# Forget-gate columns as row dot products on VectorE, from a second load of x

## The chip, the cores and the metric

One core of one Trainium2 chip. The time is that of one execution on the device, in microseconds; the profile is of one execution of its own. TensorE multiplies, VectorE (DVE), ScalarE (ACT) and GpSimd (POOL) work elementwise, and SyncE (SP) only issues DMAs. Each has an in-order queue of its own; they meet at semaphores.

## The reference

Two layers of a sequence trunk, T = 2048 tokens of width 1024, float32. What matters here:

```
h    = x * rsqrt(mean(x*x) + eps) * norm_g        # per token
proj = h @ w_in                                   # 1024 x 3972, 15 column groups
fq, fk, fv, ff, fg, r_pre, ... = split(proj, (256, 256, 256, 4, 256, 896, ...))
log_f = log_sigmoid(ff + b_f)                     # 4 columns: one forget gate per head
Ft    = cumsum(log_f, over the tokens)            # used in the first attention
...                                               # four mixers, each gated
x = x + mixed @ w_out
```

The group `ff` has four columns, at rows 768 to 771 of the transposed projection that the kernel keeps.

## The kernel before

Every layer projects first. TensorE forms `projT` (3972 x T) in tiles of 128 output columns of `w_in`. To keep float32 accuracy with the fast float32 form, weights and activations are split in a high and a low part (`w_hi`, `w_lo`, `h_hi`, `h_lo`), and each product is three matmuls (lines 147, 151 and 153). A tile is four blocks of 512 tokens, a block 8 x 3 = 24 matmuls into one of two PSUM accumulators `acc`. Class `Projector` (lines 74 to 171) has a method per engine:

- `act_load` fetches a tile's weights into `raw` (512 KB), issued by ScalarE, when `raw` is free; `act_split` rounds them to `w_hi` when the buffer `w_hi[q]` is free; `pool_weights` subtracts to `w_lo` on GpSimd (line 115).
- `pe_tile` runs the matmuls. The first one of a tile frees the other weight buffer, so the next but one tile's weights are split during it. Before each block it waits (line 143) until `acc` is free.
- `evacuate` (lines 158 to 165) copies `acc` to `stage`: a wait and a decrement for the accumulator, a wait and a decrement for the stage buffer, the copy, a drain that raises `acc_free`.
- `sp_store` writes the stage to DRAM (256 KB).

`phase_project` is the first stage of a layer. SP loads x in 16 tiles of 128 tokens into four buffers `xb` (line 214). ScalarE sums the squares and forms the factor `rst` per token (line 256 to 260), VectorE scales xb in place (line 363), TensorE turns it (line 313), VectorE applies the gain (line 371), ScalarE and GpSimd split h. Beside that run the first two weight tiles. Then comes `tiles`: on every engine the same order of six more tiles, written out by hand, the first four in a loop of two rounds, then the last one of the group `r_pre`, and then the four columns of `ff` (`R_FF`, with m = 4). In `tiles` VectorE only evacuates, GpSimd and ScalarE only prepare weights. At the end SP waits for the last stores (line 239); a barrier closes the stage.

`phase_rwkv_prep` and `phase_rwkv_scan` project the other tiles between their own work, one tile per unit, with the weight buffer alternating (`q`, `1 - q`). Their plans of how many matmuls go in at which point aren't touched. The attention and output stages follow; they read `projT` from DRAM.

## Time and profile before

| | |
|---|---|
| time, median of 3 | 3059.63 us (3056.31 to 3061.36) |
| profiled execution, first to last instruction | 3053.4 us |
| mean granted clock of TensorE | 0.978 |
| TensorE busy | 2901.2 us, 95% |
| VectorE busy | 1441.2 us, 47% |
| ScalarE busy | 1079.7 us, 35% |
| GpSimd busy | 1064.3 us, 35% |

The page gives no time of the profiled execution other than its span; the timed runs are 3 to 8 us above that span, 6.2 at the median. The first layer's `tiles` run from about 82 to 213 us of the span, the second layer's from about 1606 to 1737. Matmuls are pipelined: a record of about 0.39 us starts every 0.227 us. "DVEq" and "PEq" are waits in the engine's own queue.

### The profile page before, as it was taken

How to read it: one execution, taken by the hardware profiler on the slowest of the kernel's cores; microseconds unless marked ns; L12 is line 12 of the kernel's file. 1: busy time of each engine (PE TensorE's matmuls, PEld its weight loads, DVE VectorE, ACT ScalarE, POOL GpSimd, SP SyncE). 2: the span in 40 equal slices, each digit the busy share in tenths (PEclk: the TensorE clock that was granted, in tenths of full speed). 3: DMA queues.
4: the chain of work that ended last, by engine and by line, in shares of the span. 5: the costliest groups of instructions: out<-in, count | busy, mean ns of one | idle time of the engine just before them, and what ended most of it. 6: DMA issues, size and time to landing. Idle time of an engine off the chain costs nothing. (4 is left out here: it accounts for less than half of the span.)

```text
span 3053.4 us, 68189 instructions
## 1 busy us (share of the span) xinstructions
PE 2901.2 (95%) x26644; PEld 2137.6 (70%) x26644; DVE 1441.2 (47%) x2152; ACT 1079.7 (35%) x2188; POOL 1064.3 (35%) x998
## 2 busy tenths in 40 slices
PE   7999989999999899989989999899999998998899
PEld 6867877777777644467768678677777776444677
DVE  5117743323233387767461177432233323877674
ACT  5004433333333234633150044333333332346331
POOL 5101113355555523632151011233555555236221
PEclk9999999999999899999999999999999998999999
DMA  5225543344444341266342255433444443512663
GB/s 159 76 71 166 162 128 95 109 128 131 128 129 128 115 150 40 84 196 205 113 157 76 75 161 161 131 97 109 127 128 132 129 124 115 150 40 84 195 205 114
DMA packets 440642, 383.21 MB, mean 126 GB/s; under 512 B 130696, under 2 KB 369544, under 8 KB 440328
## 3 DMA queue, kind: packets, MB, share of 16 engines
q1 hardware_dynamic: 369576, 345.06, 37.1%
q10 hardware_dynamic: 70752, 33.85, 4.2%
q8 instruction: 211, 3.46, 0.5%
q14 instruction: 103, 0.84, 0.1%
HBM read 239.62 MB, written 139.23 MB: 124 GB/s over the span
## 5 line engine op out<-in xcount | busy, mean ns | idle before, releaser
L147 PE MATMUL ch_acc<-h_hi,ch_w_hi 128*128 128x512 f32 (+1 forms) x2032 | 813.6, 400 | 25.0 <-PEq L144 25.0
L153 PE MATMUL ch_acc<-h_hi,ch_w_lo 128*128 128x512 f32 (+1 forms) x2032 | 821.5, 404 | 0.0
L151 PE MATMUL ch_acc<-h_lo,ch_w_hi 128*128 128x512 f32 (+1 forms) x2032 | 817.7, 402 | 0.0
L147 PEld LDWEIGHTS ch_acc<-h_hi,ch_w_hi 128*128 128x128 f32 (+1 forms) x2032 | 377.6, 186 | 113.0 <-issue 29.1
L151 PEld LDWEIGHTS ch_acc<-h_lo,ch_w_hi 128*128 128x128 f32 (+1 forms) x2032 | 377.1, 186 | 95.9 <-issue 9.8
L153 PEld LDWEIGHTS ch_acc<-h_hi,ch_w_lo 128*128 128x128 f32 (+1 forms) x2032 | 376.9, 185 | 88.0 <-issue 0.3
L115 POOL TENSOR_TENSOR ch_w_lo<-ch_raw,ch_w_hi 128x1024 fp32r<-128x1024 f32 (+1 forms) x62 | 149.8, 2416 | 641.2 <-POOLq L114 641.2
L1814 ACT ACTIVATE fx_prob<-fx_ST 128x512 f32<-128x512 f32 (+3 forms) x320 | 153.9, 531 | 189.6 <-PE fx_ST L1661 95.9
L2069 PE MATMUL so_acc<-ea_wo_hi,so_m_hi 128*128 128x512 f32 x512 | 209.6, 409 | 7.5 <-DVEq L2174 3.8
L2070 PE MATMUL so_acc<-ea_wo_hi,so_m_lo 128*128 128x512 f32 x512 | 204.2, 399 | 0.0
L2071 PE MATMUL so_acc<-ea_wo_lo,so_m_hi 128*128 128x512 f32 x512 | 204.2, 399 | 0.0
L867 POOL TENSOR_SCALAR rs_qx<-rs_qx,rs_gain 128x256 f32<-128x256 f32 x112 | 103.5, 924 | 281.5 <-ACT rs_qr L1160 264.0
L164 ACT COPY ch_stage<-ch_acc 128x512 f32<-128x512 f32 x192 | 112.3, 585 | 227.8 <-ACTq L163 227.6
L1590 POOL TENSOR_TENSOR fx_sump<-fx_sump,fx_prob 128x1024 f32<-128x1024 f32 (+2 forms) x60 | 126.6, 2109 | 188.2 <-ACT fx_prob L1814 186.9
L1728 DVE TENSOR_REDUCE fx_nm<-fx_SS 128x2 f32<-128x1024 f32 (+3 forms) x160 | 166.4, 1059 | 46.9 <-PE fx_SS L1637 32.0
L164 DVE COPY ch_stage<-ch_acc 128x512 f32<-128x512 f32 (+1 forms) x64 | 44.1, 689 | 259.8 <-DVEq L163 259.8
L110 ACT ACTIVATE ch_w_hi<-ch_raw 128x1024 fp32r<-128x1024 f32 x64 | 65.9, 1029 | 243.0 <-ACTq L109 243.0
L2004 POOL TENSOR_TENSOR so_m_lo<-so_y,so_m_hi 128x512 fp32r<-128x512 f32 x58 | 79.6, 1372 | 191.7 <-ACT so_m_hi L1944 187.1
L1717 DVE TENSOR_TENSOR fx_sumd<-fx_sumd,fx_prob 128x1024 f32<-128x1024 f32 (+3 forms) x72 | 129.2, 1795 | 11.8 <-ACT fx_prob L1814 5.0
L2069 PEld LDWEIGHTS so_acc<-ea_wo_hi,so_m_hi 128*128 128x128 f32 x512 | 97.7, 191 | 35.9 <-DVEq L2174 8.4
L2071 PEld LDWEIGHTS so_acc<-ea_wo_lo,so_m_hi 128*128 128x128 f32 x512 | 97.2, 190 | 23.8
L2070 PEld LDWEIGHTS so_acc<-ea_wo_hi,so_m_lo 128*128 128x128 f32 x512 | 97.8, 191 | 21.6
(286 smaller groups left out, 4812.5 us busy)
## 6 DMA issues: line engine op xcount, KB each, us to landing
projT<-ch_stage SPq DMA_DIRECT2D x248, 256.0 KB
ch_raw<-w_in ACTq DMA_DIRECT2D x62, 512.0 KB, 5.4
pj_xb<-x SPq DMA_DIRECT2D x32, 512.0 KB, 4.2
so_stage<-x SPq DMA_DIRECT2D x64, 256.0 KB, 3.0
rp_pre<-projT SPq DMA_DIRECT2D x16, 899.5 KB, 7.6
rs_qx<-projT SPq DMA_DIRECT2D x112, 128.0 KB, 3.3
rs_cs<-rope SPq DMA_DIRECT2D x48, 256.0 KB, 3.6
so_cv<-projT SPq DMA_DIRECT2D x42, 258.0 KB, 3.8
```

What stands on the lines that cost most here:

```text
L115: (G or self.nc.gpsimd).tensor_tensor(self.w_lo[q][:, :, 0:m], self.raw[:, :, 0:m], self.w_hi[q][:, :, 0:m].bitcast(F32), ALU.subtract).th ...
L147: ins = M(acc, self.w_hi[q][:, k, 0:m], self.h_hi[:, k, cols], start=(k == 0), stop=False)
L151: M(acc, self.w_hi[q][:, k, 0:m], self.h_lo[:, k, cols], start=False, stop=False)
L153: ins = M(acc, self.w_lo[q][:, k, 0:m], self.h_hi[:, k, cols], start=False, stop=(k == KC - 1))
L164: copy(self.stage[e][0:m, :], self.acc[e][0:m, :]).then_inc(self.stage_rdy[e], 1)
L1590: G.tensor_tensor(sump[R % 2][:, :, lo:TB], sump[R % 2][:, :, lo:TB], prob[nt % NP][:, :, lo:TB], ALU.add).then_inc(s["add_p"], 1)
L1717: V.tensor_tensor(sumd[R % 2][:, :, lo:TB], sumd[R % 2][:, :, lo:TB], prob[i % NP][:, :, lo:TB], ALU.add).then_inc(s["add_d"], 1)
L1728: V.tensor_reduce(nm[p][:, :, t, c:c + 1], SS[ns % 2][:, :, 0:width(t, c)], AX.X, ALU.max, negate=True).then_inc(s["m_rdy"], 1)
L1814: A(prob[nt % NP][:, h, lo:TB], ST[h][:, lo:TB], ACT.Exp).then_inc(s["p_rdy"], 1)
L2069: M(a, m_hi[e][:, c, rows], wo_hi[:, c, cols], start=(i == 0), stop=False)
L2070: M(a, m_lo[e][:, c, rows], wo_hi[:, c, cols], start=False, stop=False)
L2071: ins = M(a, m_hi[e][:, c, rows], wo_lo[:, c, cols], start=False, stop=(i == KC - 1))
```

## The change

The small tile is gone from `tiles`, which now has five tiles, unrolled. Two new inputs are prepared on the host from the inputs: `gate_w`, the four columns of `w_in` laid out as rows of 1024, and `gains`, `norm_g` as a row. SP broadcasts both to all 128 partitions once the first pass of x is nearly through, and then loads x a second time, tile by tile, into the same four buffers. On VectorE `gate_w` is multiplied by the gain, and one `scalar_tensor_tensor` per token tile and column multiplies x by the weights and sums over the row (`accum_out`); its elementwise output goes to a PSUM tile that nobody reads. `dots_done(n)` spreads the 64 dots over blocks 1 to 18: three or four behind each evacuation. The sums are multiplied by `rst`, turned by TensorE (64 columns), copied and stored by four small DMAs into the four rows of `projT`.

Because one tile less runs, the weight buffers are exchanged from there on: `q` for `1 - q` in both later stages. The diff, without the parts that only hand the new inputs down:

```diff
@@ -190,28 +190,36 @@
         NZ = (R_RG - R_PRE) // 128
         zero = P.sb("zero", [128, NZ, PAD])
         pt = [P.ps(f"pt{q}", [128, KC, 128]) for q in two]
-        names = ("c_in", "p_in", "c_rdy", "z_st", "r_rdy", "x_rdy", "pt_rdy", "hg_rdy", "hi_rdy", "lo_rdy", "lo3_rdy")
+        gw, gr = P.sb("gw", [128, NH, DM]), P.sb("gr", [128, 1, DM])
+        fl, ft = P.sb("fl", [128, NH, NT]), P.sb("ft", [NH * NT, 128])
+        dots = P.ps("dots", [128, DM])
+        names = ("gw_in", "dot_rdy", "fl_rdy", "ft_rdy", "f_rdy", "f_st", "c_in", "p_in", "c_rdy", "z_st", "r_rdy", "x_rdy", "pt_rdy", "hg_rdy", "hi_rdy", "lo_rdy", "lo3_rdy")
         s = {n: P.sem(n) for n in names}
         x_in = [P.sem(f"x_in{q}") for q in range(NX)]
         block = ctx.enter_context(nc.Block())
         rows = [R_PRE, R_PRE + 128]
         assert NZ == 7
+        rest = [R_PRE + 128 * i for i in range(2, NZ)]
+
         def tiles(eng, body):
-
-            with eng.Fori(0, 2) as i:
-                for q in two:
-                    body(i * 256 + (R_PRE + 128 * (q + 2)), q, i * 256 + (R_PRE + 128 * (q + 3)))
-            body(R_RG - 128, 0, R_FF, 128, NH)
-            body(R_FF, 1, R_FQ, NH, 128)
+            for i, row in enumerate(rest):
+                body(row, i % 2, (rest + [R_FQ])[i + 1])
+
+        def dots_done(n):
+
+            return -(-NT * NH * n // (NB * len(rest) - 2))
         @block.sync
         def _(sp):
             def load(t):
-                if t >= NX:
+                if NX <= t < NT + NX:
                     sp.wait_ge(s["pt_rdy"], t - NX + 1)
-                sp.dma_start(xb[t % NX][:], x[t * 128:(t + 1) * 128, :]).then_inc(x_in[t % NX], 16)
+                if t >= NT + NX:
+                    sp.wait_ge(s["dot_rdy"], NH * (t - NT - NX + 1))
+                tok = t % NT * 128
+                sp.dma_start(xb[t % NX][:], x[tok:tok + 128, :]).then_inc(x_in[t % NX], 16)
             load(0)
             sp.dma_start(ident[:], consts[:, 0:128]).then_inc(s["c_in"], 16)
@@ -221,6 +229,11 @@
             for t in range(2, NT + 8):
                 if t < NT:
                     load(t)
+                if t == NT:
+                    sp.dma_start(gr[:], gains[l:l + 1].to_broadcast([128, 1, DM])).then_inc(s["gw_in"], 16)
+                    sp.dma_start(gw[:], gate_w[l:l + 1].to_broadcast([128, NH, DM])).then_inc(s["gw_in"], 16)
+                if NT < t <= NT + NX:
+                    load(t - 1)
                 if t == NT - 1 and l == 0:
                     sp.wait_ge(s["c_rdy"], 1)
                     for r0, r1 in ((R_PRE, R_RG), (R_SK, R_SG), (R_CB, R_CG)):
@@ -231,10 +244,18 @@
                     if t == BT * b + 9 + 2 * n and 0 <= b < NB:
                         J.sp_store(sp, rows[n], b, 128, n)
-            def body(row, q, follows, m=128, after=128):
+            def body(row, q, follows):
                 for b in range(NB):
-                    J.sp_store(sp, row, b, m)
+                    J.sp_store(sp, row, b)
+                    n = rest.index(row) * NB + b
+                    for t in range(NX, NT):
+                        if dots_done(n) >= NH * (t - NX + 1) > dots_done(n - 1):
+                            load(NT + t)
             tiles(sp, body)
+            sp.wait_ge(s["f_rdy"], 1)
+            for j in range(NH):
+                sp.dma_start(projT[R_FF + j:R_FF + j + 1, PAD:PAD + T].rearrange("j (t p) -> (j t) p", p=128), ft[NT * j:NT * (j + 1), :]).then_inc(s["f_st"], 16)
+            sp.wait_ge(s["f_st"], 16 * NH)
             for q in two:
                 sp.wait_ge(J.stage_st[q], 16)
             if nz:
@@ -281,11 +302,11 @@
                 if t == 8:
                     J.act_load(act, R_PRE + 256)
-            def body(row, q, follows, m=128, after=128):
-                J.act_split(act, q, m)
-                J.act_load(act, follows, after)
+            def body(row, q, follows):
+                J.act_split(act, q)
+                J.act_load(act, follows)
             tiles(act, body)
-            J.act_split(act, 0)
+            J.act_split(act, 1)
         @block.gpsimd
         def _(pool):
@@ -298,8 +319,8 @@
                 pool.drain().then_inc(s["lo_rdy"], 1)
                 if t == 4:
                     J.pool_weights(pool, 1)
-            tiles(pool, lambda row, q, follows, m=128, after=128: J.pool_weights(pool, q, m))
-            J.pool_weights(pool, 0)
+            tiles(pool, lambda row, q, follows: J.pool_weights(pool, q))
+            J.pool_weights(pool, 1)
         @block.tensor
         def _(pe):
@@ -345,10 +366,12 @@
             for _ in tile[1]:
                 pass
-            def body(row, q, follows, m=128, after=128):
-                for _ in J.pe_tile(pe, q, m):
+            def body(row, q, follows):
+                for _ in J.pe_tile(pe, q):
                     pass
             tiles(pe, body)
+            pe.wait_ge(s["fl_rdy"], 1)
+            nc.tensor.transpose(dots[0:NH * NT, 0:128], fl[:].rearrange("p j t -> p (j t)"), ident[:]).then_inc(s["ft_rdy"], 1)
         @block.vector
         def _(v):
@@ -380,10 +403,30 @@
                     if t == BT * b + 7 + 2 * n and 0 <= b < NB:
                         J.evacuate(v, V.tensor_copy, b, 128, n)
-            def body(row, q, follows, m=128, after=128):
+            def dot(n):
+                t, j = divmod(n, NH)
+                if j == 0:
+                    v.wait_ge(x_in[t % NX], 16 * ((NT + t) // NX + 1))
+                V.scalar_tensor_tensor(dots[:], xb[t % NX][:], 1.0, gw[:, j], ALU.mult, ALU.mult, accum_out=fl[:, j, t:t + 1])
+                v.drain().then_inc(s["dot_rdy"], 1)
+
+            def body(row, q, follows):
                 for b in range(NB):
-                    J.evacuate(v, V.tensor_copy, b, m)
+                    J.evacuate(v, V.tensor_copy, b)
+                    n = rest.index(row) * NB + b
+                    if n == 0:
+                        v.wait_ge(s["gw_in"], 32)
+                        for j in range(NH):
+                            V.tensor_tensor(gw[:, j], gw[:, j], gr[:, 0], ALU.mult)
+                        v.drain()
+                    for i in range(min(dots_done(n - 1) if n else 0, NT * NH), min(dots_done(n), NT * NH)):
+                        dot(i)
+                    if n == NB * len(rest) - 2:
+                        V.tensor_tensor(fl[:], fl[:], rst[:].rearrange("p (o t) -> p o t", o=1).to_broadcast([128, NH, NT]), ALU.mult)
+                        v.drain().then_inc(s["fl_rdy"], 1)
             tiles(v, body)
+            v.wait_ge(s["ft_rdy"], 1)
+            V.tensor_copy(ft[:], dots[0:NH * NT, 0:128]).then_inc(s["f_rdy"], 1)
 PREP_FILL = (("th", 16), ("lora", 24), ("ssk", 20), ("bs", 36))
...
-                J.act_split(act, 1 - q)
+                J.act_split(act, q)
...
-            units(pool, lambda i, q, row, follows: J.pool_weights(pool, 1 - q))
+            units(pool, lambda i, q, row, follows: J.pool_weights(pool, q))
-                tile = J.pe_tile(pe, q)
+                tile = J.pe_tile(pe, 1 - q)
...
-                            J.pool_weights(pool, (t + 1) % 2)
+                            J.pool_weights(pool, t % 2)
...
+        "gate_w": np.ascontiguousarray(a["w_in"][:, :, R_FF:R_FF + NH].transpose(0, 2, 1)), "gains": a["norm_g"][:, None, :],
```

## Rows read from the trace of the kernel before

The timeline's rows give the start, the length, the engine, the line, the operation with output <- input, and in brackets the idle time ahead and what ended it. A queue's own name (DVEq, PEq) stands for a wait in it.

**Rows 1.** The page: engines' busy time, and TensorE's granted clock in 40 slices.

```profile
PE 2901.2 (95%) x26644; PEld 2137.6 (70%) x26644; DVE 1441.2 (47%) x2152; ACT 1079.7 (35%) x2188; POOL 1064.3 (35%) x998
...
PEclk9999999999999899999999999999999998999999
```

**Rows 2.** Stretches: length, busy us (instructions) of five engines, granted clock, DMA share, GB/s.

```profile
87.80:109.60 21.80, 21.80 (x97) 18.04 (x97) 2.78 (x5) 1.06 (x1) 4.19 (x2) 1.00 0.23 74
...
191.10:213.40 22.30, 22.01 (x96) 7.87 (x93) 2.76 (x5) 1.06 (x1) 2.41 (x1) 1.00 0.03 13
...
216.70:220.40 3.70, 3.64 (x10) 2.84 (x11) 0.00 (x0) 1.01 (x1) 0.00 (x0) 0.56 0.70 215
```

**Rows 3.** Timeline, DVE: start us, length us, line, tiles, [idle before it].

```profile
87.83 0.69 DVE L164 COPY ch_stage<-ch_acc 128x512 f32<-128x512 f32 x1 [4.75 <-DVEq L163]
93.26 0.69 DVE L164 COPY ch_stage<-ch_acc 128x512 f32<-128x512 f32 x1 [4.75 <-DVEq L163]
...
191.18 0.69 DVE L164 COPY ch_stage<-ch_acc 128x512 f32<-128x512 f32 x1 [4.75 <-DVEq L163]
196.73 0.68 DVE L164 COPY ch_stage<-ch_acc 4x512 f32<-4x512 f32 x1 [4.86 <-DVEq L163]
...
213.37 0.68 DVE L164 COPY ch_stage<-ch_acc 4x512 f32<-4x512 f32 x1 [4.87 <-DVEq L163]
```

**Rows 4.** Groups of DVE by shape: count | busy us, mean ns | idle us.

```profile
L371 DVE TENSOR_TENSOR pj_hg<-pj_pt,pj_pars 128x1024 f32<-128x1024 f32 x32 | 39.1, 1221 | 22.4 <-PE pj_pt L313 21.9 <-issue 0.4
...
L2155 DVE SCALAR_TENSOR_TENSOR so_g<-ea_vs,so_g 128x1024 f32<-128x1024 f32 x16 | 18.9, 1222 | 1.2
...
L533 DVE COPY rp_pend<-rp_lw 128x8 f32<-128x8 f32 x16 | 2.6, 164 | 0.0
```

**Rows 5.** Timeline, DVE, where a drain or a wait lies between instructions.

```profile
224.27 2.03 DVE L495 TENSOR_TENSOR rp_dif<-rp_pre 128x1792 f32<-128x1792 f32 x1 [0.20 <-DVEq L494]
226.49 2.86 DVE L500 SCALAR_TENSOR_TENSOR rp_xs<-rp_dif,rp_pars,rp_pre 128x256 f32<-128x256 f32 x7 [0.20 <-DVEq L498]
229.49 0.62 DVE L506 TENSOR_SCALAR rp_kkr<-rp_xs,rp_pars 128x256 f32<-128x256 f32 x2
230.18 0.69 DVE L508 TENSOR_TENSOR rp_dif<-rp_kkr 128x512 f32<-128x512 f32 x1
```

**Rows 6.** Timeline, DVE, two large instructions merged.

```profile
2856.18 2.36 DVE L2155 SCALAR_TENSOR_TENSOR so_g<-ea_vs,so_g 128x1024 f32<-128x1024 f32 x2
```

**Rows 7.** Timeline, ACT: a sum over the row and its read-out.

```profile
59.78 1.04 ACT L256 ACTIVATE pj_sq<-pj_xb 128x1024 f32<-128x1024 f32 x1
60.73 0.19 ACT L256 ACTIVATION_READ_ACCUMULATOR pj_sq<-pj_xb 128x1 f32 x1
60.98 0.29 ACT L258 ACTIVATE pj_rst<-pj_ms,pj_eps 128x1 f32<-128x1 f32 x1
```

**Rows 8.** Timeline, POOL beside the stage.

```profile
87.19 2.40 POOL L115 TENSOR_TENSOR ch_w_lo<-ch_raw,ch_w_hi 128x1024 fp32r<-128x1024 f32 x1 [6.51 <-POOLq L114]
105.48 2.40 POOL L115 TENSOR_TENSOR ch_w_lo<-ch_raw,ch_w_hi 128x1024 fp32r<-128x1024 f32 x1 [15.89 <-POOLq L114]
```

**Rows 9.** Timeline, all engines, where POOL and DVE meet.

```profile
241.41 0.69 DVE L538 SCALAR_TENSOR_TENSOR rp_ta<-rp_cmp,rp_kkr 128x512 f32<-128x512 f32 x1
...
241.61 2.72 POOL L115 TENSOR_TENSOR ch_w_lo<-ch_raw,ch_w_hi 128x1024 fp32r<-128x1024 f32 x1 [46.68 <-POOLq L114]
...
242.02 2.87 DVE L539 SCALAR_TENSOR_TENSOR rp_tb<-rp_ta,rp_kkr 128x512 f32<-128x512 f32 x1
```

**Rows 10.** Timeline, SP and TensorE at the end of the stage, first layer.

```profile
214.14 0.25 SPq L171 DMA_DIRECT2D projT<-ch_stage  x1
216.42 0.42 SPq L449 DMA_DIRECT2D rp_pre<-projT  x1
...
216.76 0.47 PE L147 MATMUL ch_acc<-h_hi,ch_w_hi 128*128 128x512 f32 x1 [3.65 <-PEq L144]
```

**Rows 11.** Line 214, the loads of x: issues, and their time to landing.

```profile
DMA to landing us min/median/max: 3.2/4.2/6.6
```

More of the change, by code:

```diff
@@ L171, in sp_store, with phase_project @@
         sp.dma_start(self.projT[bass.ds(r, m), PAD + b * TB:PAD + (b + 1) * TB], self.stage[e][0:m, :]).then_inc(self.stage_st[e], 16)
-def phase_project(nc, l, x, par, consts, projT, h_hi, h_lo, J):
+def phase_project(nc, l, x, par, gate_w, gains, consts, projT, h_hi, h_lo, J):
     with ExitStack() as ctx:
@@ L979, in body @@
             def body(t, row, e):
-                tile = J.pe_tile(pe, e)
+                tile = J.pe_tile(pe, 1 - e)
                 def fill(stage):
@@ L1196, in body @@
                 if nxt is not None:
-                    J.act_split(act, 1 - e)
+                    J.act_split(act, e)
                 for sa, xa, f1, f2 in (("s6a", "x4_a", "s6", "s7"), ("s8a", "x5_a", "s8", "s9")):
@@ L2198, in _, with hybrid_trunk @@
                 add_x(n, 3)
-def hybrid_trunk(nc, x, w_in, w_out, par, lora, consts, masks, rope, out, layers=L, debug=None):
+def hybrid_trunk(nc, x, w_in, w_out, par, gate_w, gains, lora, consts, masks, rope, out, layers=L, debug=None):
     def dram(n, shape):
@@ L2214, in hybrid_trunk @@
                 J = Projector(Phase(nc, ctx, f"ch{l}", closes=False), nc, l, w_in, h_hi, h_lo, projT)
-                phase_project(nc, l, source, par, consts, projT, h_hi, h_lo, J)
+                phase_project(nc, l, source, par, gate_w, gains, consts, projT, h_hi, h_lo, J)
                 phase_rwkv_prep(nc, l, projT, par, lora, consts, rw, pend, J)
```

## The prediction

> **What bounds the kernel now.** The first view is the page: TensorE is busy 95% of the span, VectorE 47% [rows 1], and its granted clock is at the higher of its two levels (2.4 GHz) nearly throughout. Time leaves this kernel where TensorE's queue becomes shorter, or comes back where TensorE is made to wait. The second view is the table of stretches. In a stretch of full projection tiles TensorE is busy for all 21.80 us at clock 1.00 while VectorE works 2.78; in the stretch of the four-column tile, 22.30 us, it is still busy for 22.01 us [rows 2]. So four output columns cost what 128 cost. The third view is VectorE in order of time, which is the metronome of this stage: one evacuation per block of 512 tokens, 5.44 us apart (87.83, 93.26, ..., 191.18: 19 steps, 103.35 us), and 5.55 us apart in the small tile [rows 3]. Between two of them VectorE idles 4.75 us. The question is whether the new work goes into those gaps.
>
> **What is removed.** Per layer the four blocks of the small tile: from the evacuation at 191.18 to that at 213.37, 22.19 us [rows 3]. All of it is TensorE's own time, none beside other work. Its load, split and store go too, at no value, since all ran beside TensorE. The unrolled loop and the exchanged buffer indices (0 for 1) in the later stages I cost at nothing: the same instructions in the same order, and blocks inside and outside the loop have the same pace.
>
> **What one dot costs.** 64 dots per layer (16 token tiles, 4 columns), each one VectorE instruction over 128x1024 with both inputs in SBUF, its sum written out, and a drain behind it. The nearest row is a scalar_tensor_tensor of 128x1024 with both inputs in SBUF: 1.222 us [rows 4]. A drain that raises a semaphore costs 0.14 (226.49 + 2.86 = 229.35, the next starts at 229.49), a plain one 0.07 (229.49 + 0.62 = 230.11, then 230.18) [rows 5]. No row shows VectorE handing out a sum, and none shows it writing to PSUM; reading from PSUM costs nothing (1.221) [rows 4]. On ScalarE the read-out is an instruction of 0.19 that starts 0.09 before the end of the main one, so it adds 0.10 [rows 7]. VectorE's small copy takes 0.164 [rows 4] and, started as early, would add 0.08. Bounds: 1.22 + 0.07 = 1.29 if the read-out is inside and the drain cheap, 1.22 + 0.19 + 0.14 = 1.55 if the read-out overlaps nothing. I take 1.39: 1.22 + 0.14 + 0.03, near the lower end, since a read-out has no input to fetch.
>
> The Trainium skill, "VectorE: DVE Perf Modes", section "Two Vector instructions with no wait between them", says that an instruction which also writes its accumulator out is really two. VectorE's rows here cannot show it; ScalarE's two rows look just so. By a full small instruction the dot would be 1.44.
>
> **What VectorE has to do between 93.26 and 191.18 (97.9 us), per layer.**
> - 64 dots x 1.39 = 89.0.
> - 18 evacuations (blocks 1 to 18). Each is 0.69, with 0.14 for its drain behind it; ahead of it stand two waits with two decrements, which hid in idle time so far and now follow a drain. A drain with one wait and one decrement takes 0.20 (226.30 to 226.49) against 0.07 for a drain, so a pair is 0.12 and two are 0.24 [rows 5]. 1.07 x 18 = 19.3. Bounds 0.83 and 1.2 each.
> - The four products weights x gain at block 0: four of 128x1024, 1.14 apart (2.36 - 1.22) [rows 6]. They want SBUF while GpSimd holds it from 87.19 to 89.59 [rows 8], so they run from 89.59 to about 94.3, and the evacuation of block 1 starts 1.2 us late.
> - GpSimd's low weight parts, four more of 2.40 us inside this time, the first at 105.48 [rows 8]. Where both meet, the one that comes second waits for the whole of the other: GpSimd takes 2.72 in place of 2.40 behind L538, and L539, otherwise 0.69, takes 2.87, ending 0.6 after GpSimd [rows 9]. Between 0 and 2.4 each; an evacuation reads PSUM and can run beside it, so I take 1.4, 5.6 in all.
> - The product with the row factors at the end, 0.35.
>
> Sum 89.0 + 19.3 + 1.2 + 5.6 + 0.35 = 115.4, and 115.4 - 97.9 = 17.5 us more than the time there is. VectorE becomes the bound of this stage: its evacuations fall behind by about 0.9 us per block; from about 4.6 us of delay on (a block of 5.44 less the evacuation), TensorE stands waiting for an accumulator. The delay doesn't vanish in that slack, since the last evacuation and the last dots stand in VectorE's one queue, and the stage ends with them. So the stage ends 17.5 us later than its 20 blocks would let it.
>
> **The end of the stage.** Today: last evacuation at 213.37, its store issued at 214.14 for 0.25, next stage's first issue at 216.42 [rows 10]: 2.0 us for landing and barrier. New: the same evacuation, then a copy of the turned sums, then four small stores in a row on SP, of 0.42 us each as L449 takes there [rows 10], then the same 2.0: 3.05 becomes about 5.0. I take 1.95 more; bounds 0.8 (the issues overlap the copy) and 3. TensorE's turn of 64 columns hides in the wait. TensorE waits 3.65 us now and then runs at 0.56 of its clock for the stretch of 3.7 us [rows 10, 2]; with a longer wait I put 0.8 on that, between 0 and 2.
>
> **The second load of x**, 16 x 512 KB on SP, is costed at nothing: a load lands in 4.2 us, 6.6 at most [rows 11], is issued some 12 dots (17 us) ahead, and the DMA engines are 0.23 busy [rows 2]. SP waits for dots between two stores, but those dots stand ahead of the next evacuation on VectorE anyway. The broadcast weights (2.5 MB, at about 60 us) have 30 us. If that cover fails the first dots start late, by a few us at most.
>
> **Sum.** Per layer -22.2 + 17.5 + 1.95 + 0.8 = -1.95; two layers -3.9. The profiled span of 3053.4 becomes 3049.5; with the 6.2 us between that span and the median, 3055.7.
>
> **Rivals.**
> - VectorE keeps up (dot 1.30, evacuation 0.9, GpSimd costing 0.5 each). Then 83.2 + 16.2 + 1.2 + 2 + 0.35 - 97.9 = 5.1; -22.2 + 5.1 + 2 + 0.5 = -14.6 per layer, 3030. For it: the rows of undisturbed instructions. Against it: the drain, which I read from a row.
> - On the other side: the dot itself is heavier, read-out in full, 1.55. The only price that counts is the dot's: break-even lies at 1.39 + 1.95/64 = 1.42. At 1.55 it is +10.2 - 1.95 = +8.3 per layer, 3076. For it: ScalarE's read-out of 0.19; against it: that one overlaps.
> - The dot runs at half rate, if two SBUF inputs and the sum get in each other's way. Rows of 1024 and 512 columns (1.22 and 0.69) give 1.06 more. 64 x 1.06 = 68 per layer: +66, so 3192. Against it: the same form without a sum runs at 1.222 [rows 4].
> - The loads don't do what they should (weights or tiles late, a store held back on SP). Each first dot late by 2 us more adds 2 us per layer, as VectorE has no idle time left to make it up: -3.9 + 4 = 0, 3060. Against it: the landing times.
>
> To the third: the Trainium skill, "Vector Engine (DVE) Microarchitecture Reference", section "Points that are easy to get wrong", says that this form with two non-bf16 SBUF sources halves its throughput, as no port is left to read the accumulator back. The row of 1.222 us disagrees for an instruction without a sum; no row here shows one with it.
>
> **Numbers.** Forecast 0.50, VectorE keeps up 0.20, heavier dot 0.20, half rate 0.07, loads 0.03. The likeliest case has its own range, 3046 to 3068: a dot of 1.34 gives 3049, one of 1.47 gives 3066, and the other terms widen it. What a measurement can tell from no change is about 0.2%, 6 us. The forecast gives faster 0.18, same 0.31, slower 0.01; keeping up gives 0.20 faster; the heavier dot 0.17 slower, 0.03 same; half rate slower; loads same. Together 0.38, 0.37, 0.25. The range 3029 to 3080 leaves out half rate and the edges of two others.
>
> **What would show it.** Evacuations between blocks 1 and 19 about 6.4 us apart in the mean instead of 5.44, VectorE busy over 90% there; the dots' start-to-start distance 1.39, or what it is; GpSimd's four instructions beside dots of 2.5 us and more; TensorE waiting at L144 from the second tile on; 5 us from the last evacuation to the next stage. I am wrong if VectorE still idles before each evacuation (then it is about 3030), or if dots are over 1.42 apart (then slower).

## The result, and the profile after

| | before | changed |
|---|---|---|
| time, medians on one chip | 3059.61 us (12 runs) | 3062.23 us (12 runs, 3059.17 to 3068.86) |
| ratio, 95% interval | | 1.0017 [1.001, 1.0024] |
| second measurement | 3055.93 (29 runs) | 3060.38 (11 runs), 1.0008 [0.9999, 1.0017] |
| profiled span, mean granted clock | 3053.4, 0.978 | 3063.7, 0.973 |

By the medians the change costs 2.6 us in one measurement and 4.5 in the other, where a gain of 3.9 was forecast. The ratio with its interval is an estimate of its own, not the quotient of the two medians: by it the cost is 5.2 us (3.1 to 7.3) and 2.4 us (-0.3 to 5.2), so the first measurement shows a loss clear of noise and the second by itself does not. The time is inside the range (3029 to 3080) and on the other side of before. The 10 us between the two spans are not the result: single executions of one kernel spread over more than that.

The page of the changed kernel: busy times, the granted clock, the costliest matmul group and the group of the new dots. A group's columns are as in [rows 4].

```profile
PE 2870.1 (94%) x26454; PEld 2126.7 (69%) x26454; DVE 1626.6 (53%) x2412; ACT 1079.8 (35%) x2186; POOL 1069.7 (35%) x996
...
PEclk9999999999999899989989899999999998999899
...
L147 PE MATMUL ch_acc<-h_hi,ch_w_hi 128*128 128x512 f32 x1968 | 793.7, 403 | 51.5 <-PEq L144 51.5
...
L410 DVE SCALAR_TENSOR_TENSOR pj_dots<-pj_xb,pj_gw 128x1024 f32<-128x1024 f32 x128 | 172.3, 1346 | 16.6 <-issue 1.0
```

TensorE is busy for 31.1 us less than in [rows 1]. The small tiles had been 44; in the next view the 19 steps hold 107.18 and 108.04 us of its busy time, where they were 103.35 us without a gap before. At L147 it now waits 51.5 us for accumulators and stage starts (25.0 before). VectorE is busy 53% of the span, which says nothing of the stage that matters. The next view shows that: the stretches from the evacuation of block 0 to that of block 19, first and second layer, columns as in [rows 2].

```profile
88.56:212.75 124.19, 107.18 (x456) 85.66 (x454) 108.85 (x152) 4.24 (x4) 12.23 (x5) 0.98 0.34 108
1621.04:1743.38 122.34, 108.04 (x456) 86.93 (x454) 107.38 (x152) 4.25 (x4) 12.47 (x5) 0.97 0.34 110
```

Before, the same 19 steps took 103.35 us [rows 3]. They now take 20.8 and 19.0 us more, and the busier engine is VectorE: 108.85 of 124.19 us, drains and waits in its queue not counted.

The timeline of VectorE in this stage, first layer. A DVE_READ_ACCUMULATOR row is the read-out of the sum, an instruction of its own.

```profile
88.56 0.69 DVE L164 COPY ch_stage<-ch_acc 128x512 f32<-128x512 f32 x1 [4.75 <-DVEq L163]
89.39 5.01 DVE L420 TENSOR_TENSOR pj_gw<-pj_gw,pj_gr 128x1024 f32<-128x1024 f32 x4
94.70 0.69 DVE L164 COPY ch_stage<-ch_acc 128x512 f32<-128x512 f32 x1 [0.30 <-DVEq L163]
95.53 1.23 DVE L410 SCALAR_TENSOR_TENSOR pj_dots<-pj_xb,pj_gw 128x1024 f32<-128x1024 f32 x1
96.68 0.14 DVE L410 DVE_READ_ACCUMULATOR pj_dots<-pj_xb,pj_gw 128x1 f32 x1
96.94 1.23 DVE L410 SCALAR_TENSOR_TENSOR pj_dots<-pj_xb,pj_gw 128x1024 f32<-128x1024 f32 x1
...
99.76 1.24 DVE L410 SCALAR_TENSOR_TENSOR pj_dots<-pj_xb,pj_gw 128x1024 f32<-128x1024 f32 x1
101.40 0.69 DVE L164 COPY ch_stage<-ch_acc 128x512 f32<-128x512 f32 x1 [0.34 <-DVEq L163]
102.22 1.23 DVE L410 SCALAR_TENSOR_TENSOR pj_dots<-pj_xb,pj_gw 128x1024 f32<-128x1024 f32 x1
...
106.46 3.23 DVE L410 SCALAR_TENSOR_TENSOR pj_dots<-pj_xb,pj_gw 128x1024 f32<-128x1024 f32 x1
...
212.19 0.22 DVE L425 TENSOR_TENSOR pj_fl<-pj_fl,pj_rst 128x64 f32<-128x64 f32 x1
212.75 0.69 DVE L164 COPY ch_stage<-ch_acc 128x512 f32<-128x512 f32 x1 [0.34 <-DVEq L163]
```

Here the prices can be read. From one dot's start to the next it is 96.94 - 95.53 = 1.41: 1.15 to the read-out, 0.14 for it, 0.12 for the drain. An evacuation among dots adds 102.22 - 101.17 = 1.05 (99.76 + 1.41 = 101.17), with 0.34 idle ahead of it where 4.75 were [rows 3]. The dot at 106.46 took 3.23 instead of 1.23, since GpSimd had started first:

```profile
106.20 2.39 POOL L115 TENSOR_TENSOR ch_w_lo<-ch_raw,ch_w_hi 128x1024 fp32r<-128x1024 f32 x1 [16.30 <-POOLq L114]
```

The end of the stage, on SP and on TensorE:

```profile
213.53 0.32 SPq L171 DMA_DIRECT2D projT<-ch_stage  x1
213.90 1.81 SPq L257 DMA_DIRECT2D projT<-pj_ft  x4
217.63 0.39 SPq L492 DMA_DIRECT2D rp_pre<-projT  x1
```

```profile
212.49 0.42 PE L374 MATMUL pj_dots<-pj_ident,pj_fl 128*64 128x128 f32 x1 [5.32 <-DVEq L426]
217.98 0.77 PE L147 MATMUL ch_acc<-h_hi,ch_w_hi 128*128 128x512 f32 x1 [5.07 <-PEq L144]
```

From the last evacuation to the next stage's first issue it is 217.63 - 212.75 = 4.88, and in the second layer 6.37, where the four small stores took 3.15 to issue. It was 3.05 [rows 3, 10] and, in the second layer, 3.21. TensorE waits twice, 5.32 us for the last sums and 5.07 for the next stage, where it waited once for 3.65 [rows 10].

### The profile page after: what moved, and what is told of

Same layout as the page of the kernel before. It is cut to its first block and busy times, and to the rows that moved or that the text cites. A ratio compares the mean times of both kernels' runs of the same rounds, so it can differ in the third digit from the quotient of the medians.

```text
span 3063.7 us, 68038 instructions
## 1 busy us (share of the span) xinstructions
PE 2870.1 (94%) x26454; PEld 2126.7 (69%) x26454; DVE 1626.6 (53%) x2412; ACT 1079.8 (35%) x2186; POOL 1069.7 (35%) x996
## 5 line engine op out<-in xcount | busy, mean ns | idle before, releaser
L147 PE MATMUL ch_acc<-h_hi,ch_w_hi 128*128 128x512 f32 x1968 | 793.7, 403 | 51.5 <-PEq L144 51.5
L153 PE MATMUL ch_acc<-h_hi,ch_w_lo 128*128 128x512 f32 x1968 | 799.7, 406 | 0.0
L151 PE MATMUL ch_acc<-h_lo,ch_w_hi 128*128 128x512 f32 x1968 | 796.2, 405 | 0.0
L147 PEld LDWEIGHTS ch_acc<-h_hi,ch_w_hi 128*128 128x128 f32 x1968 | 374.0, 190 | 135.6 <-issue 60.7
L151 PEld LDWEIGHTS ch_acc<-h_lo,ch_w_hi 128*128 128x128 f32 x1968 | 374.1, 190 | 87.0 <-issue 9.8
L153 PEld LDWEIGHTS ch_acc<-h_hi,ch_w_lo 128*128 128x128 f32 x1968 | 373.3, 190 | 79.6 <-issue 0.3
L115 POOL TENSOR_TENSOR ch_w_lo<-ch_raw,ch_w_hi 128x1024 fp32r<-128x1024 f32 x60 | 153.1, 2552 | 640.7 <-POOLq L114 640.7
L410 DVE SCALAR_TENSOR_TENSOR pj_dots<-pj_xb,pj_gw 128x1024 f32<-128x1024 f32 x128 | 172.3, 1346 | 16.6 <-issue 1.0
```

Of the source, the lines that this page charges most:

```text
L115: (G or self.nc.gpsimd).tensor_tensor(self.w_lo[q][:, :, 0:m], self.raw[:, :, 0:m], self.w_hi[q][:, :, 0:m].bitcast(F32), ALU.subtract).th ...
L147: ins = M(acc, self.w_hi[q][:, k, 0:m], self.h_hi[:, k, cols], start=(k == 0), stop=False)
L151: M(acc, self.w_hi[q][:, k, 0:m], self.h_lo[:, k, cols], start=False, stop=False)
L153: ins = M(acc, self.w_lo[q][:, k, 0:m], self.h_hi[:, k, cols], start=False, stop=(k == KC - 1))
L410: V.scalar_tensor_tensor(dots[:], xb[t % NX][:], 1.0, gw[:, j], ALU.mult, ALU.mult, accum_out=fl[:, j, t:t + 1])
```

## The experiments

Theory A is the prediction's mechanism: VectorE's queue has more work than time, the stage ends with it, the loads of x cost nothing. The rivals put the cost into the loads or into the clock behind the stage (theory C). "Steps" are the 19 steps from block 0 to block 19, first layer; "end" is from the last evacuation to the next stage's first issue, both layers. Kernels with the same time in the column "kernel before" ran on one chip together, and a median is compared with another best inside such a group.

| kernel | median | kernel before | ratio | steps | end |
|---|---|---|---|---|---|
| changed | 3060.38 | 3055.93 | 1.0008 [0.9999, 1.0017] | 124.74 | 4.87, 5.02 |
| no reload | 3061.94 | 3055.93 | 1.0019 [1.001, 1.0029] | 124.39 | 4.88, 5.56 |
| extra matmuls | 3054.42 | 3055.93 | 0.9992 [0.9983, 1.0001] | 124.48 | 4.91, 5.05 |
| one drain for four dots | 3021.21 | 3055.93 | 0.988 [0.9865, 0.9894] | 105.11 | 5.00, 5.02 |
| no dots | 3018.33 | 3055.40 | 0.987 [0.9854, 0.9887] | 103.36 | 4.88, 5.02 |
| small low parts | 3048.98 | 3055.40 | 0.9979 [0.9969, 0.9989] | 117.99 | 4.88, 5.01 |
| ScalarE evacuates | 3021.91 | 3055.40 | 0.9882 [0.9865, 0.9898] | | 4.82, 4.92 |
| the same, one store | 3020.39 | 3055.40 | 0.9884 [0.9867, 0.99] | | 4.12, 4.20 |
| no sum | 3055.96 | 3058.68 | 0.999 [0.9981, 0.9999] | 118.92 | 4.88, 5.02 |
| one store, again | 3021.14 | 3058.68 | 0.9871 [0.9856, 0.9887] | | 4.12, 4.20 |
| one store, extra matmuls | 3012.25 | 3058.68 | 0.985 [0.9837, 0.9864] | | 4.12, 4.19 |
| before, extra matmuls | 3058.48 | 3057.14 | 1.0002 [0.9993, 1.0011] | 103.35 | 3.15, 3.30 |

**Without the dots.** Loads, products, drains, turn and stores stay, and the sums stay zero.

```diff
-                V.scalar_tensor_tensor(dots[:], xb[t % NX][:], 1.0, gw[:, j], ALU.mult, ALU.mult, accum_out=fl[:, j, t:t + 1])
```

> Leaves the 64 dots per layer out (the forget gates' sums stay zero), all else as in the changed kernel: second load of x, the products weights x gain, the turn, the four small stores, the unrolled tiles. Theory A (VectorE's queue bounds the stage): without the dots the evacuations are back at 5.44 us apart and on time, so per layer the 20.8 us (first layer) and 19.0 us (second layer) of delay go, and part of the 4 to 5 us of low clock behind the stage: 3062 - 40 - 5 = about 3018, 3010 to 3025. Theory B (the gain is lost in what else was added: loads, longer end of the stage, exchanged buffers, unrolled code): within 10 us of the changed kernel, 3052 to 3062.

Measured: 3018.33, 37.1 us faster than before; the steps are 103.36, the 103.35 of [rows 3] again, and the end is still 4.88. So all the lateness belongs to the dots in VectorE's queue. Two small tiles are 44.4 us, and 7.3 of them are not recovered: 3.6 of these are the longer ends (4.88 and 5.02 for 3.05 and 3.21), and the other 3.7 are not located; the interval of the ratio alone is 10 us wide.

**The loads of x.** The dots read the first four token tiles again and again; the second load stops there.

```diff
                 if t >= NT + NX:
-                    sp.wait_ge(s["dot_rdy"], NH * (t - NT - NX + 1))
+                    return
...
-                if j == 0:
+                if j == 0 and t < NX:
                     v.wait_ge(x_in[t % NX], 16 * ((NT + t) // NX + 1))
```

> 12 of the 16 second loads of x per layer are left out (the dots of later tiles read the first four again), 12 MB of DMA less. Theory A: only the two short waits of VectorE that stand at the head of a tile (0.5 us together) go: 0 to 2 us less than the changed kernel. Rival D (the loads cost time: SP's queue, DMA shared with the stores and weights, low landing): 5 us or more less.

Measured: 3061.94, not faster than the changed kernel's 3060.38, with steps of 124.39. The 12 loads that are left out are free, as costed. The short wait that I had put on a load stays, at the same dot as in the changed kernel (137.16 there), though this dot waits for no load:

```profile
137.33 1.23 DVE L410 SCALAR_TENSOR_TENSOR pj_dots<-pj_xb,pj_gw 128x1024 f32<-128x1024 f32 x1 [0.50 <-issue]
```

So it isn't the loads; what it is, no run shows.

**GpSimd's part.** In four of the tiles GpSimd forms only 4 of the 128 columns of the low part.

```diff
-            tiles(pool, lambda row, q, follows: J.pool_weights(pool, q))
+            tiles(pool, lambda row, q, follows: J.pool_weights(pool, q, 128 if row == rest[0] else NH))
```

> GpSimd makes the low weight part of only 4 of 128 columns for four of the tiles in the stage (the other columns keep old low parts), so the four instructions of 2.4 to 3.0 us beside the dots become short. The dots that met them took 3.2 us in place of 1.23: 2.0 us x 4 per layer. Theory A: the stage ends 7.8 us earlier per layer, VectorE still late by 12: 3062 - 15.6 = 3046, 3041 to 3050. Rival: the meeting costs nothing because the delay is made up elsewhere (TensorE or the loads bound the stage): 3060 to 3064.

Measured: 3048.98; steps 117.99, 6.2 to 6.8 less than the changed kernel's. The group of the dots in this kernel shows where it comes from: their mean falls from 1346 to 1264 ns.

```profile
L410 DVE SCALAR_TENSOR_TENSOR pj_dots<-pj_xb,pj_gw 128x1024 f32<-128x1024 f32 x128 | 161.8, 1264 | 16.6 <-issue 1.0
```

128 x 0.082 us is 10.5 us, 5.2 per layer. Of the four meetings between blocks 1 and 19 only three went: the fourth instruction of GpSimd is still whole here (175.90 for 3.01 us) and its dot takes 3.17. The fourth short one stood beside the products at block 0, which are no longer late. 3 x 1.9 + 0.7 = 6.4 is about what the steps lost, less than the 7.8 that I expected. The meetings are real and of the size that the timeline shows.

**One drain for four dots.** The elementwise output of the four goes to four different tiles, as they no longer wait for each other, and only the last has a drain.

```diff
-                V.scalar_tensor_tensor(dots[:], xb[t % NX][:], 1.0, gw[:, j], ALU.mult, ALU.mult, accum_out=fl[:, j, t:t + 1])
-                v.drain().then_inc(s["dot_rdy"], 1)
+                V.scalar_tensor_tensor((dots[:], sq[:], hg[0][:].rearrange("p k c -> p (k c)"), hg[1][:].rearrange("p k c -> p (k c)"))[j], xb[t % NX][:], 1.0, gw[:, j], ALU.mult, ALU.mult, accum_out=fl[:, j, t:t + 1])
+                if j == NH - 1:
+                    v.drain().then_inc(s["dot_rdy"], NH)
...
                         v.wait_ge(s["gw_in"], 32)
+                        v.wait_ge(s["lo_rdy"], NT - 1)
```

> One drain per token tile (4 dots) in place of one per dot; the elementwise outputs go to four buffers that are idle by then. Theory A: each of 48 drains that go per layer saves its 0.12 at least, 5.8 us, up to 0.2 if the read-out also overlaps: the dot's pitch falls from 1.41 to 1.29 or lower, and the time by 11 to 19 us: 3042 to 3050 if the changed kernel is at 3061. Rival (pitch set by the read-out and the pipeline, the drain hidden in it): no change.

Measured: 3021.21, 39.2 us less than the changed kernel, where I expected 11 to 19. VectorE's timeline of this kernel says why:

```profile
93.94 1.23 DVE L410 SCALAR_TENSOR_TENSOR pj_dots<-pj_xb,pj_gw 128x1024 f32<-128x1024 f32 x1
95.09 0.14 DVE L410 DVE_READ_ACCUMULATOR pj_dots<-pj_xb,pj_gw 128x1 f32 x1
95.09 1.22 DVE L410 SCALAR_TENSOR_TENSOR pj_sq<-pj_xb,pj_gw 128x1024 f32<-128x1024 f32 x1
...
107.71 1.21 DVE L410 SCALAR_TENSOR_TENSOR pj_sq<-pj_xb,pj_gw 128x1024 f32<-128x1024 f32 x1
108.86 0.07 DVE L410 DVE_READ_ACCUMULATOR pj_sq<-pj_xb,pj_gw 128x1 f32 x1
108.86 1.21 DVE L410 SCALAR_TENSOR_TENSOR pj_hg<-pj_xb,pj_gw 128x1024 f32<-128x1024 f32 x1
110.00 0.08 DVE L410 DVE_READ_ACCUMULATOR pj_hg<-pj_xb,pj_gw 128x1 f32 x1
110.00 0.68 DVE L164 COPY ch_stage<-ch_acc 128x512 f32<-128x512 f32 x1
```

Without a drain the next instruction starts where the read-out starts: 108.86 - 107.71 = 1.15 instead of 1.41. The other output buffers are not the reason: the dot at 93.94 still writes to PSUM, and its successor starts 1.15 later too. An evacuation behind such a dot starts at once: 110.00 - 108.86 = 1.14 after the dot's start, against 101.40 - 99.76 = 1.64 behind a drained one. 12 evacuations of this layer stand so. With 36 dots that are followed by a dot, undrained, that is 36 x 0.26 + 12 x 0.5 = 15.4 us. The meetings with GpSimd cost less too, 2.5 us in this layer: the four dots take 2.16, 2.85, 2.36 and 2.77. The short waits of 0.85 us are gone. The steps take 105.11 instead of 124.74, 19.6 less, of which these terms are 18.7. Most of VectorE's 21 us too much was the drain with its semaphore behind each dot, its own time and the wait that it lays before the next evacuation. I had expected less, because I priced a drain at 0.12 to 0.2 and saw neither the evacuations nor the meetings in it. No run has the drain without its semaphore.

**No sum.** The same instruction with no accumulator output.

```diff
-                V.scalar_tensor_tensor(dots[:], xb[t % NX][:], 1.0, gw[:, j], ALU.mult, ALU.mult, accum_out=fl[:, j, t:t + 1])
+                V.scalar_tensor_tensor(dots[:], xb[t % NX][:], 1.0, gw[:, j], ALU.mult, ALU.mult)
```

> The 64 instructions per layer without their sum (no read-out; the forget gates' sums stay zero), drain and output as before. In the changed kernel instruction, read-out and drain take 1.41 from start to start: 1.15 to the read-out, 0.14, 0.12. Theory A: without it 1.23 + 0.12 = 1.35, so 0.06 x 64 = 3.8 us less per layer, 7.7 in all. Rival (the sum makes the whole instruction slower): more than 15 us less.

Its timeline shows four drained products in one row:

```profile
95.66 5.29 DVE L411 SCALAR_TENSOR_TENSOR pj_dots<-pj_xb,pj_gw 128x1024 f32<-128x1024 f32 x4
```

(5.29 - 1.23) / 3 = 1.35 apart: the sum costs 0.06 of the 1.41. Steps 118.92, 5.3 to 5.8 less; 64 x 0.06 = 3.8 of it is the sum, 0.9 is how the products met GpSimd (6.9 us over the four meetings, 7.8 with the sum), and the short waits of 0.85 are not there. The time, 2.7 us less than before where the changed kernel was 2.6 to 4.5 more, fits the 7.7 expected; the two did not run in one group.

**ScalarE evacuates the 20 blocks**, one tile behind its own weight work; VectorE keeps only the dots.

```diff
+                if row == rest[0]:
+                    act.wait_ge(s["front"], 1)
+                else:
+                    for b in range(NB):
+                        J.evacuate(act, nc.scalar.copy, b)
...
                 for b in range(NB):
-                    J.evacuate(v, V.tensor_copy, b)
```

> In the stage's 20 blocks ScalarE (busy 1.06 us of 21.8 there) takes the evacuations; VectorE has only the dots. Theory A: VectorE's queue loses 18 x 1.05 us of evacuations, about 19 us, and nothing of TensorE's chain stands behind a dot: dots from about 90 to 189, the 20 blocks end at 191.5. Per layer the removed tile is worth its 22.2 less about 2 for the longer end and 0 to 3 for clock: 3059.6 - 2 x 19 = 3021, 3014 to 3027. Rival: ScalarE's own queue (the split waits for GpSimd, which waits for dots) makes the evacuations late, as VectorE's did: over 3035.

Measured: 3021.91, as expected: with nothing of TensorE's chain behind the dots, 33.5 of the 44.4 us that were taken out are gained, and 3.5 of the rest are the longer ends. With the four small stores as one:

```diff
-            for j in range(NH):
-                sp.dma_start(projT[R_FF + j:R_FF + j + 1, PAD:PAD + T].rearrange("j (t p) -> (j t) p", p=128), ft[NT * j:NT * (j + 1), :]).then_inc(s["f_st"], 16)
+            sp.dma_start(projT[R_FF:R_FF + NH, PAD:PAD + T].rearrange("j (t p) -> j t p", p=128), ft[:]).then_inc(s["f_st"], 16)
```

> As e3_act_evac, and the four small stores at the end are one DMA. Three issues of 0.45 us less per layer on SP at the end of the stage: 1.3 us x 2 below e3_act_evac, 3018. Rival: the large last store lands later than the small ones anyway: equal to e3_act_evac.

> The same kernel as e3b_act_evac_one_store, with more rounds, beside e9: 0.988 of the kernel before.

Measured: 3020.39 and, again, 3021.14; the end is 0.7 us shorter (4.12), about half of what I had put on it. The medians (3021.91 and 3020.39) can't tell the two kernels apart. In this kernel the row product runs 3 us ahead of the last evacuation, now on ScalarE, and the small store issues right behind the large one:

```profile
190.88 0.58 ACT L164 COPY ch_stage<-ch_acc 128x512 f32<-128x512 f32 x1 [4.85 <-ACTq L163]
```

```profile
187.82 0.23 DVE L432 TENSOR_TENSOR pj_fl<-pj_fl,pj_rst 128x64 f32<-128x64 f32 x1
```

```profile
191.55 0.32 SPq L171 DMA_DIRECT2D projT<-ch_stage  x1
191.92 0.68 SPq L256 DMA_DIRECT2D projT<-pj_ft  x1
195.00 0.39 SPq L499 DMA_DIRECT2D rp_pre<-projT  x1
```

The store's issue fell from 1.81 to 0.68, and the end by only 0.7. That the landing, not the issue, sets most of the end is how I read it; no run takes them apart.

**The clock behind the stage.** The changed kernel with 20 unread matmuls ahead of TensorE's wait for the sums and 18 behind the turn.

```diff
+            def extra(count):
+                for _ in range(count):
+                    nc.tensor.matmul(pt[0][:, 0:4, :], J.w_hi[0][:, 0, :], J.h_hi[:, 0, 0:TB], start=True, stop=True)
+            extra(20)
             pe.wait_ge(s["fl_rdy"], 1)
             nc.tensor.transpose(dots[0:NH * NT, 0:128], fl[:].rearrange("p j t -> p (j t)"), ident[:]).then_inc(s["ft_rdy"], 1)
+            extra(18)
```

> The changed kernel with 20 and 18 matmuls that nobody reads, put where TensorE waits at the end of the stage: 20 before its wait for the sums (5.3 us idle there in the changed kernel), 18 behind the turn (5.1 us idle until the next stage). Question: the granted clock behind the stage is low for 6.8 us of lost TensorE time per layer, against 1.4 and 3.2 in the kernel before, and 1.7 to 3.4 where TensorE waits only once. Theory C (part of the loss is clock, and it follows from TensorE's waiting): the lost time at the stage's end falls from 6.8 to 3 or less per layer, and the time by 2 x 3 to 2 x 5: 6 to 10 us less than the changed kernel, so it would be below the kernel before. Rival (the clock falls there whatever TensorE does, or the lost clock is hidden by waits for loads in the next stage): within 2 us of the changed kernel.

Measured: 3054.42, 6.0 us less than the changed kernel beside it. Two stretches of 20 us behind the ends of the stage (granted clock is the third number from the right), first of the changed kernel of the same measurement, then with the extra matmuls:

```profile
210.00:230.00 20.00, 13.09 (x51) 10.15 (x51) 8.88 (x18) 2.17 (x3) 0.00 (x0) 0.74 0.51 162
1735.00:1755.00 20.00, 12.55 (x47) 9.78 (x49) 8.79 (x19) 2.17 (x3) 0.00 (x0) 0.69 0.50 152
```

```profile
210.00:230.00 20.00, 17.20 (x78) 13.15 (x76) 7.64 (x16) 3.48 (x7) 0.00 (x0) 1.00 0.50 152
1735.00:1755.00 20.00, 17.66 (x80) 13.55 (x79) 8.68 (x19) 3.39 (x7) 0.00 (x0) 1.00 0.49 152
```

In the changed kernel the granted clock is a mixture of 2.4 and 1.2 GHz (0.74 and 0.69); with matmuls in place of the waits it is at 2.4 GHz throughout. Part of the stretch is waiting, and a low clock costs no time where nothing runs. What it costs is seen in TensorE's first matmuls behind the stage: at the low clock one starts every 0.43 us instead of every 0.227. The first matmul of the next stage, one of the slow ones and the first of that stage's own (L652), first layer of the changed kernel of this measurement; then the first and the last of these with the extra matmuls, where none is slow:

```profile
217.33 0.77 PE L147 MATMUL ch_acc<-h_hi,ch_w_hi 128*128 128x512 f32 x1 [5.06 <-PEq L144]
220.88 0.63 PE L153 MATMUL ch_acc<-h_hi,ch_w_lo 128*128 128x512 f32 x1
229.02 0.48 PE L652 MATMUL rp_pw<-rp_dif,rp_up 64*128 64x256 f32 x1
```

```profile
216.69 0.47 PE L147 MATMUL ch_acc<-h_hi,ch_w_hi 128*128 128x512 f32 x1 [1.08 <-PEq L144]
227.43 0.45 PE L657 MATMUL rp_pw<-rp_dif,rp_up 64*128 64x256 f32 x1 [0.94 <-issue]
```

From the first to the L652 matmul it is 11.69 and, in the second layer, 11.79; with the extra matmuls 10.74 and 9.73. So 3.0 us of the 6.0 are gained there, and the steps of the second layer took back 1.5 (123.94 for 122.42). Where the rest comes from, the traces do not show.

The control is the kernel before with 12 of these matmuls at its stage's end:

> The kernel before, with 12 matmuls that nobody reads at the end of its stage, where it idles 3.65 and 3.8 us. Control for e8 and e9. Theory C: the lost clock there (1.4 and 3.2 us in its profile) goes, 3 to 5 us less than the kernel before, 0.9985; the changed kernel lost more there only because it waits twice and longer. Rival (the matmuls help only behind VectorE's lateness): no change, 1.000.

Measured: 3058.48 against 3057.14, ratio 1.0002. The clock behind the stage is 1.00 here too, and no time was gained. The same stretches of the kernel before itself:

```profile
210.00:230.00 20.00, 16.35 (x68) 11.31 (x67) 6.26 (x12) 2.77 (x5) 0.00 (x0) 0.91 0.45 138
1735.00:1755.00 20.00, 16.19 (x61) 11.92 (x60) 7.06 (x13) 3.12 (x6) 0.00 (x0) 0.83 0.52 163
```

Behind its stage 10 and 14 matmuls are slow, in the changed kernel 10 and 10. From the first behind the stage to the L609 matmul (L652 in the changed kernel) it is 11.34 and 12.57 before, against 11.69 and 11.79 there. With the 12 extra matmuls it is 9.74 and 10.84, so 3.3 us are gained at this place as well, and yet the time is the same. So the extra matmuls make the changed kernel faster, by 6.0 us in the medians and 4.9 by the two ratios, which is measured; that the clock behind the stage is the reason is not shown, and still less that the change has made it worse.

**Together:** ScalarE evacuates, one store, 12 extra matmuls behind the turn.

> ScalarE evacuates, one small store, and 12 matmuls that nobody reads behind TensorE's turn at the end of the stage, where it is idle for 4.6 us. Theory C (clock follows from waiting): the 1.7 us of lost clock per layer behind the stage goes, 3.4 us less than the same kernel without them (e3c): about 0.987 of the kernel before. Rival: no change, since one wait of 1 to 2 us more or less is not what the clock falls on.

Measured: 3012.25, 46.4 us faster than before, and faster than both kernels of this case. It is 8.9 us less than one store alone (3021.14; 5 and 4 runs), where 3.4 were expected, and the traces place only 1.1 of them between block 0's evacuation and the first matmul of the next stage's own. In the first layer the 12 matmuls did not keep the clock up:

```profile
196.51 0.57 PE L147 MATMUL ch_acc<-h_hi,ch_w_hi 128*128 128x512 f32 x1 [1.82 <-PEq L144]
199.44 0.63 PE L151 MATMUL ch_acc<-h_lo,ch_w_hi 128*128 128x512 f32 x1
```

This is the second sign that the gain of such matmuls is not understood here.

## Why the forecast came out on the wrong side

The mechanism was the right one: VectorE became the bound of this stage, its lateness reached the end in full, and it took back nearly all of the 22.2 us per layer. A gain of 1.95 per layer was the difference of terms ten times as large. The step that failed is the size of the largest: how late VectorE is. The three terms, per layer:

- **VectorE late: 17.5 put, 20.8 and 19.0 measured.** In the first layer: dots 64 x 1.41 = 90.2 (89.0 put); evacuations 18 x 1.05 = 18.9 (19.3 put); products 0.7 late (1.2 put); meetings with GpSimd 3.23 + 3.15 + 3.16 + 3.16 - 4 x 1.23 = 7.8 (5.6 put); row product 0.34 (0.35 put); and 0.85 of short waits, one ahead of a dot (0.50, of unknown cause) and one for an accumulator (0.35 more than the usual 0.34), which had no term. Sum 118.8, less the 97.9 there are: 20.9. In the second layer the meetings are 6.7 (2.10 + 3.15 + 3.16 + 3.16 - 4 x 1.23) and the products are 0.3 late, which gives the 19.0. The changed kernel of the second measurement has 21.4 and 19.1. The largest error is the meetings: I counted on an evacuation taking some of them, but a dot stood there each time.
- **The end of the stage: 1.95 put, 1.8 and 3.2 measured** (4.88 - 3.05 and 6.37 - 3.21). Right in the first layer and in both layers of the second measurement (4.87, 5.02), 1.2 too small in one stage end of four.
- **The clock: 0.8 put, 1.05 and 0.0 measured**, and 0.35 and -0.8 in the second measurement. This is how much longer it takes than before from the first matmul behind the stage to the L652 matmul: 12.39 and 12.59, then 11.69 and 11.79, against 11.34 and 12.57. TensorE does wait twice now, but the kernel before ran its first matmuls behind the stage slowly too. The term was not too small.

These terms can be added up against the trace. The rows are the first matmul of L609 before, then of L652 in the changed kernel, each in both layers:

```profile
228.10 0.48 PE L609 MATMUL rp_pw<-rp_dif,rp_up 64*128 64x256 f32 x1
1752.76 0.48 PE L609 MATMUL rp_pw<-rp_dif,rp_up 64*128 64x256 f32 x1
```

```profile
230.37 0.48 PE L652 MATMUL rp_pw<-rp_dif,rp_up 64*128 64x256 f32 x1
1762.68 0.48 PE L652 MATMUL rp_pw<-rp_dif,rp_up 64*128 64x256 f32 x1
```

| from block 0's evacuation to this matmul | first layer | second layer | both, against before |
|---|---|---|---|
| before | 140.27 | 141.67 | |
| changed | 141.81 | 141.64 | +1.5 |
| changed, second measurement | 141.65 | 139.57 | -0.7 |
| forecast | | | -3.9 |

In the first layer -22.2 + 20.8 + 1.8 + 1.05 = +1.5, in the second -22.2 + 19.0 + 3.2 + 0.0 = 0.0, and the trace says +1.54 and -0.03. So the lateness of VectorE, 20.1 in the mean of four instead of 17.5, takes 5.2 us for two layers, more than the forecast gain of 3.9; the end took 0.4 more and the clock 1.3 less.

The two measurements lie on both sides of what these terms give together (-3.9 + 5.2 + 0.4 - 1.3 = +0.4). That leaves about 1 us (2.6 less 1.5) and 5 us (4.5 and 0.7) of the medians outside this part of the kernel, and no run places them. Everything outside it took 2771.5 us in the profiled execution before, 2780.3 and 2778.1 in those of the changed kernel, but also 2779.5 in the kernel before with its 12 extra matmuls: single executions differ there by more than what is sought. The unrolled loop is cleared by the steps of 103.36 without dots; the exchanged weight buffers in the later stages, costed at nothing, were never tested alone. So the traces show why the gain did not come; that the time went up by a few us stays unexplained in part.

The break-even that the prediction gave, a dot of 1.42, was met by a dot of 1.41, so the rival "heavier dot" (1.55) did not happen. The prediction said there that the only price that counts is the dot's, and that was a fault: the dots' own price was 1.2 of the 3.4 us that the first layer was off. A margin of 0.03 per dot was 1.95 us, and the GpSimd term, put at 5.6, had bounds of 0 to 9.6, with the upper end 4 us away. The forecast's own range reached 3068, but the chance of slower should have been the larger one.

Right: the read-out on top of the dot (the 1.15 + 0.14 + 0.12 add to 1.41 against 1.39), the wait pair of an evacuation, the free loads, that VectorE would be too late, that TensorE waits at L144 in the stage:

```profile
PE ch_acc L147 <- PEq L144: 16.8, 9, 5.1
PE pj_dots L374 <- DVEq L426: 5.3, 1, 5.3
```

(waits of TensorE from 60 to 240 us: total us, times, longest; 5.07 of the 16.8 are the next stage's start; before it was one of 3.7.)

"VectorE keeps up" at 3030 was not wrong in kind either: with one drain for four dots it nearly does (1.8 us late), at 3021.

The half-rate rival fell. The dots run at 1.23 with the sum, the same as the 1.222 without one [rows 4]. The Trainium skill, "Vector Engine (DVE) Microarchitecture Reference", section "Points that are easy to get wrong", states the halving for this form; 128 rows here disagree. The Trainium skill, "VectorE: DVE Perf Modes", section "The DRAIN you can't avoid", says that a semaphore behind each copy costs nothing extra over one behind the last. These runs have an explicit drain with each semaphore, and there it does cost: 1.41 against 1.15 a dot.

## What to carry to other kernels

When an engine goes from idle to fully loaded, price the drains first: each one costs its own time, the overlap with the next instruction, and the idle time that the waits behind it need. If it ends a sum that nobody reads until later, one drain for several is enough. Where the forecast is a small difference of large terms, hold the margin against the bounds of all its terms together, not of the one that seems to carry it. And to price a clock, count the slow instructions behind a stage in the trace of before as well as after: a low share over a stretch that is partly waiting says little.

## What was not expected of the hardware

- A read-out costs VectorE almost nothing if no drain follows: the next instruction starts with it (108.86), and with the drain it costs 0.06 of 1.41 (1.35 without a sum).
- The elementwise output of a dot may go to PSUM or SBUF: 1.15 from start to read-out in both (95.53 to 96.68; 107.71 to 108.86).
- A dot that starts 0.26 us behind a GpSimd instruction of 2.39 us loses 2.0 us: 3.23 instead of 1.23 (106.20 and 106.46).
- 20 + 18 matmuls whose results nobody reads made a kernel 6.0 us faster, of which 3.0 are seen behind the stage; 12 of them in another gained 3.3 at the same place and nothing in the time.
